# A feed-forward stage on one core: gate-up products in seven block products instead of eight, down projections in a second half

## What is computed

```python
h = h + mixed @ w_out
hn = rms_norm(h, ffn_norm_g)
h = h + (silu(hn @ w_ffn_gate) * (hn @ w_ffn_up)) @ w_ffn_down     # 1024 -> 2816 -> 1024
y = rms_norm(h, final_norm_g)
```

## Time and profile before

| what | us |
|---|---|
| median of 3 runs (3351.07 to 3356.76) | 3355.32 |
| the profiled execution's own time | 3351.76 |
| its span in the trace | 3350.0 |

### The profile page before, as it was taken

How to read it: one execution, slowest core, us unless ns; L and a number is a source line. 1 busy time by engine, 2 the same in 40 slices (tenths; PEclk the granted TensorE clock), 3 DMA queues, 4 the chain that set the end, 5 groups by cost and what they waited for, 6 DMA issues and landing times.

```text
span 3350.0 us, 48536 instructions
## 1 busy us (share of the span) xinstructions
PE 3205.6 (96%) x19989; PEld 2651.2 (79%) x19989; DVE 1698.0 (51%) x3486; ACT 1203.4 (36%) x2403; POOL 548.2 (16%) x797
## 2 busy tenths in 40 slices
PE   8999999999999989899889999899999999999998
PEld 6888888888887767787667788778888788888886
DVE  3544445354454736536653898676653343334234
ACT  4542443344344433323452132566622311111113
POOL 0230131122022513203342132000020000000000
PEclk9999999999999989999989999999999999999999
DMA  3113112211311021131112132100043311111111
GB/s 104 39 39 120 38 46 73 72 33 53 111 65 39 20 91 45 70 138 33 51 66 77 58 94 82 45 1 1 1 176 114 120 51 51 44 45 51 51 51 51
DMA packets 59479, 210.12 MB, mean 63 GB/s; under 512 B 7015, under 2 KB 11721, under 8 KB 54522
## 3 DMA queue, kind: packets, MB, share of 16 engines
q1 hardware_dynamic: 59258, 207.02, 17.7%
HBM read 161.91 MB, written 45.09 MB: 62 GB/s over the span
## 4 chain that ended last, share of the span: by engine, by line
PE 88%; DVE 4%; ACT 4%; POOL 2%; issue 1%; DMA 1%; SPq 0%; POOLq 0%; DVEq 0%; ACTq 0%
PE pp L632 11%; PE pp L633 11%; PE pp L635 11%; PE pp L1238 9%; PE pp L1239 9%; PE pp L1240 9%; PE pp L805 2%; PE pp L807 2%; PE pp L806 2%; PE pp L1211 2%; PE pp L1195 2%; PE pp L763 1%; PE pp L733 1%; PE pp L747 1%; PE pp L1203 1%
## 5 line engine op out<-in xcount | busy, mean ns | idle before, releaser
L632 PE MATMUL pp<-gx_hi,pw_hi 128*128 128x512 f32 x1504 | 616.0, 410 | 22.0 <-DVE pw_lo L1955 22.0
L635 PE MATMUL pp<-gx_hi,pw_lo 128*128 128x512 f32 x1504 | 593.5, 395 | 0.0
L633 PE MATMUL pp<-gx_lo,pw_hi 128*128 128x512 f32 x1504 | 593.1, 394 | 0.0
L632 PEld LDWEIGHTS pp<-gx_hi,pw_hi 128*128 128x128 f32 x1504 | 286.8, 191 | 87.4 <-DVE pw_lo L1955 22.7
L635 PEld LDWEIGHTS pp<-gx_hi,pw_lo 128*128 128x128 f32 x1504 | 286.2, 190 | 62.7
L633 PEld LDWEIGHTS pp<-gx_lo,pw_hi 128*128 128x128 f32 x1504 | 287.2, 191 | 55.1
L1238 PE MATMUL pp<-mix_hi,wt_hi 128*128 128x512 f32 x704 | 274.1, 389 | 2.8 <-DVE arena L2616 1.6
L1239 PE MATMUL pp<-mix_lo,wt_hi 128*128 128x512 f32 x704 | 273.9, 389 | 0.0
L1240 PE MATMUL pp<-mix_hi,wt_lo 128*128 128x512 f32 x672 | 261.4, 389 | 0.0
L1928 ACT ACTIVATE xT<-pp 128x1024 f32<-128x1024 f32 x22 | 22.6, 1029 | 535.3 <-PE pp L1240 535.3
L2648 DVE TENSOR_TENSOR xT<-xT,pp 128x1024 f32<-128x1024 f32 x22 | 26.9, 1221 | 368.7 <-ACT xT L1928 368.7
(11 more groups left out here) (510 smaller groups left out, 6819.9 us busy)
## 6 DMA issues: line engine op xcount, KB each, us to landing
arena<-in_tiles_dram SPq DMA_DIRECT2D x73, 512.0 KB, 3.5
arena<-in_units_dram SPq DMA_DIRECT2D x33, 1024.0 KB, 4.8
y_scratch<-y SPq DMA_DIRECT2D x48, 512.0 KB, 2.9
y<-y_scratch SPq DMA_DIRECT2D x40, 512.0 KB, 4.4
xT<-in_tiles_dram SPq DMA_DIRECT2D x27, 512.0 KB, 4.2
xT<-in_w_outs_dram SPq DMA_DIRECT2D x12, 1024.0 KB, 7.1
arena<-gates_scratch SPq DMA_DIRECT2D x16, 512.0 KB, 3.7
xT<-in_wall_dram SPq DMA_DIRECT2D x3, 2048.0 KB, 9.7
```

The lines of the kernel that those rows point to most:

```text
L632: mm(b[:, hs], wh[:, c], X[0][:, k, hs], k == 0, False)
L633: m = mm(b[:, hs], wh[:, c], X[1][:, k, hs], False, both and k == 7)
L635: m = mm(b[:, hs], wl[:, c], X[0][:, k, hs], False, k == 7)
```

## The change

Each gate-up tile is a product of 2x2 blocks: the weights are A11 and A12 (gate, first and second 512 inputs) and A21 and A22 (up), the activations B11, B12 (first 512 inputs, first and second 512 tokens) and B21, B22. Winograd's form of Strassen's scheme makes it of seven block products, each 4 x 3 = 12 matmuls into one bank, with sums before and after:

- weights, VectorE, per tile, 128x512 each: ssum = A21+A22, a21 := A11-A21, a11 := ssum-A11, a12 := A12-a11
- activations, once, on quarters of 256 tokens (128x4x256): T1 = B12-B11 (VectorE), T3 = B22-B12, T2 = B22-T1, T4 = B21-T2 (GpSimd), then all split into high and low parts
- results, per tile, 128x512 each: ScalarE copies products 1 and 5 out of PSUM; VectorE forms U2, U3, both gates and the near up; GpSimd adds U2 to the far gate and U3 to the copy of product 5
- each tile's result goes raw through DRAM (`a_scratch`); the down projections run after all tiles, in 22 steps of 48 matmuls (11 pairs for tokens 0 to 511, then 11 for 512 to 1023), and sum over the 11 pairs in eight PSUM banks

The diff, cut to its core ("..." marks what is left out):

```diff
 def unit_plan():
-    plan = [("gu", 0)]
...
+    return [("gu", j) for j in range(FF_TILES)] + [("dn", i) for i in range(FF_TILES // 2)]
...
+        products = {1: (W_first, 0, "B11", 0), 2: (W_first, 512, "B21", 0), 5: (W_sum, 0, "T1", 1), 3: (W_rest, 512, "B22", 1),
+                    6: (W_rest, 0, "T2", 2), 4: (W_rest, 1536, "T4", 2), 7: (W_rest, 1024, "T3", 3)}
...
         def pe_program(e):
...
+            def product(j, p):
+                left, c, right, spot = products[p]
+                i = ([2, 3, 0, 1] if j % 2 == 0 else [4, 5, 6, 7])[spot]
+                if p in (1, 5, 6, 7):
+                    place_(Ring([i]), ("gb", j, spot), {1: ("c11", j), 5: ("c13", j), 6: ("c21", j), 7: ("u3", j)}[p])
+                pe.wait_ge({1: ("wlA", j), 2: ("wlA", j), 5: ("wl1", j), 6: ("wlS", j, 0), 3: ("wlS", j, 0), 7: ("wlS", j, 1),
+                            4: ("wlS", j, 1)}[p])
+                pe.wait_ge({2: ("p1c", j), 3: ("p5c", j), 4: ("u2", j)}.get(p))
+                pe.wait_ge([("tl", right, 0), ("tl", right, 1)] if right[0] == "T" or right == "B22" else None)
+                for k in range(4):
...
+                    m = passes(bank[i], left[j % 2], [a[:, k, :] for a in BP[right]], slice(c + k * 128, c + k * 128 + 128),
+                               slice(0, 512), k == 0, k == 3)
+                m.then_inc(*did("gp", j, p))
+            product(0, 1)
+            product(1, 1)
+            turn(7)
+            product(0, 2)
+            product(1, 2)
+            product(0, 5)
+            product(1, 5)
+            for j in range(2):
+                for p in (7, 3, 6, 4):
+                    product(j, p)
+            for j in range(2, FF_TILES):
+                for p in (1, 5, 6, 7, 2, 3, 4):
+                    product(j, p)
+            def down(s):
+                th, i = divmod(s, ff_steps // 2)
+                pe.wait_ge(("dal", s), ("dwl", s))
...
         def act_program(e):
...
+            def down_high(s):
+                i = s % (ff_steps // 2)
+                ac.wait_ge(("al", s), ("gp", 20, 4) if s == 0 else [("a", 21, 0), ("a", 21, 1), ("c22", 21)] if s == 1 else step_end(s - 2))
+                act(a_parts[s % 2][0], a_place[s % 2], ACT.Copy).then_inc(*did("dah", s))
+                ac.wait_ge(("unit", FF_TILES + i), ("gp", 20, 4) if s == 0 else ("gp", 21, 4) if s < 3 else step_end(s - 3))
+                act(w_parts[s % 3][0], w_place[i], ACT.Copy).then_inc(*did("dwh", s))
...
+                if n == 7:
+                    first_high(1)
...
+            token_high("T1", 0)
+            copy_1(0)
+            sum_high(0)
+            token_high("B22", 0)
+            copy_1(1)
+            token_high("T3", 0)
+            rest_high(0, 1)
+            rest_high(0, 0)
+            token_high("T1", 1)
...
+            for s in range(ff_steps):
+                if s + 1 < ff_steps:
+                    down_high(s + 1)
+                if s % (ff_steps // 2) == ff_steps // 2 - 1:
+                    for n in range(4):
+                        final(s // (ff_steps // 2) * 4 + n)
...
         def dve_program(e):
...
+            def second(j):
+                dv.wait_ge(("p1c", j), ("gp", j, 6), ("a", j - 1, 0) if j else [("hf", 7), ("hst", 7)])
+                tt(U2, P1c[j % 2], at("gb", j, 2), ALU.add).then_inc(*did("u2", j))
+            def near_(j):
+                dv.wait_ge(("gp", j, 4), ("u3", j), ("c12", j))
+                tt(U2, U3, at("gb", j, 2), ALU.add).then_inc(*did("c21", j))
...
+            token_low("T1", 0)
+            sum_low(0)
+            first_sum(1)
+            token_low("B22", 0)
+            turn(7)
+            token_first(1)
+            token_low("T1", 1)
+            sum_low(1)
+            token_low("T3", 0)
+            rest_low(0, 1)
+            rest_low(0, 0)
+            token_low("B22", 1)
+            token_low("T3", 1)
+            token_low("T2", 0)
+            token_low("T2", 1)
+            other_sums(1)
+            token_low("T4", 0)
+            token_low("T4", 1)
+            second(0)
+            third(0)
+            rest_low(1, 1)
+            rest_low(1, 0)
+            far_gate(0)
+            near_gate(0)
+            near_(0)
+            far(0)
...
+            for j in range(2, FF_TILES):
+                more = j + 1 < FF_TILES
+                if more:
+                    first_low(j + 1)
+                    first_sum(j + 1)
+                    other_sums(j + 1)
+                    sum_low(j + 1)
+                second(j)
+                if more:
+                    rest_low(j + 1, 0)
+                third(j)
+                if more:
+                    rest_low(j + 1, 1)
+                else:
+                    down_low(0)
+                near_gate(j)
+                far_gate(j)
+                near_(j)
+                far(j)
...
         def pool_program(e):
...
-            for n in range(8):
+            for n in range(7):
                 rms(n)
+            token_third(0)
+            rms(7)
+            token_second(0)
+            token_fourth(0)
+            token_third(1)
+            token_second(1)
+            token_fourth(1)
+            for j in range(FF_TILES):
+                far_gate(j)
+                far_up(j)
...
         def sp_program(e):
...
+            used(0)
+            unit(2)
+            for j in range(FF_TILES):
+                if j + 1 < FF_TILES:
+                    used(j + 1)
+                    unit(j + 3)
+                if j == FF_TILES - 1:
+                    sp.wait_ge(("gp", j, 4))
+                    unit(24)
+                    a_in(1)
+                store(j)
+                if j == FF_TILES - 2:
+                    a_in(0)
```

More of the change, by code:

```diff
@@ L460, in program, with four @@
-        AA = [[over(f"a{i}_{c}", 1024, F32R, base, o + j * 1024) for j, c in enumerate(("hi", "lo"))]
-              for i, (base, o) in enumerate((("w1", 0), ("w1", 2048), ("xT", 0)))]
-        sg = [SL[0][:, 2048 + i * 1024:3072 + i * 1024] for i in range(2)]
-        order = unit_plan()
-        last_aa = [over(f"al_{c}", 1024, F32R, "arena", 13696 + (len(order) - 2) % 2 * 2048 + j * 1024) for j, c in enumerate(("hi", "lo"))]
-        def halves_of(j):
-            return last_aa if j == FF_TILES - 1 else AA[j % 3]
+        def four(name, base, at):
+            return by_four(over(name, 2048, F32R, base, at))
@@ new lines, in by_four @@
+        def by_four(a):
+            return a.rearrange("p (k t) -> p k t", k=4)
+        BP = {"B11": [a[:, 0:4, 0:512] for a in (MH, ML)], "B21": [a[:, 4:8, 0:512] for a in (MH, ML)],
+              "T1": [a[:, 0:4, 512:1024] for a in (MH, ML)], "B22": [a[:, 4:8, 512:1024] for a in (MH, ML)]}
+        for name, base in (("T3", "w2"), ("T2", "w3"), ("T4", "w1")):
+            BP[name] = [four(name + "_hi", base, 0), four(name + "_lo", base, 2048)]
+        near, far = (slice(0, 512), slice(512, 1024))
@@ new lines, in program @@
+        BR_raw = {"T1": (0, near), "T2": (0, near), "T3": (0, far), "T4": (1, near), "B22": (1, far)}
+        W_first = [[over(f"wa{i}_{c}", 1024, F32R, base, o + j * 1024) for j, c in enumerate(("hi", "lo"))]
+                   for i, (base, o) in enumerate((("arena", 8192), ("xT", 4096)))]
+        W_sum = [[over(f"w1{i}_{c}", 512, F32R, "xT", 6144 + i * 1024 + j * 512) for j, c in enumerate(("hi", "lo"))] for i in range(2)]
+        W_rest = [[over(f"ws{i}_{c}", 2048, F32R, base, j * 2048) for j, c in enumerate(("hi", "lo"))]
+                  for i, base in enumerate(("w0", "xT"))]
@@ L589, in program, with step_end @@
         attn_done = [("ot", 63), ("ao", 31), ("oT", 63), ("aT", 31), ("oa", 31)]
[L590 to L597, removed]
+        mixed = ("m2", 7, 1)
+        def step_end(s):
+            return ("dn", 0, 3, 1) if s == ff_steps // 2 - 1 else ("ds", s)
+        xs_done = [("xsl", k) for k in range(8)]
         def pe_program(e):
@@ L1284, in pe_program @@
             mix_order(mix1, turn, mix2, skip)
[L1288 to L1302, removed]
@@ L1314, in down @@
[L1314 to L1320, removed]
+                            c = x_ * 512 + n * 128
+                            m = passes(bank[2 * n + hf], a_parts[s % 2], w_parts[s % 3], slice(c, c + 128), slice(o, o + 512),
+                                       i == 0 and x_ == 0, i == ff_steps // 2 - 1 and x_ == 1)
@@ L1854, in rms, with split_x @@
             def rms(n):
+                if n == 7:
+                    first_high(1)
                 rms_rows(n, yrow[n % 2], hnf[n % 2], ff_tiny[n % 2], "hf", ("y3", n, 0), ("y3", n, 1), ("hfT", n - 2, 1) if n >= 2 else ("mix", 7))
[L1857 to L1864, removed]
+            def split_x(k):
+                ac.wait_ge([("xf", n, k // 4) for n in range(4)], ("m2", 3, 1))
+                act(xs[0][0][:, k, :], xk[k][:, 0:512], ACT.Copy).then_inc(*did("xsh", k))
@@ new lines, in token_high @@
+            def token_high(name, q):
+                x_, c = BR_raw[name]
```

(37 more changed lines are left out.)

268 lines of the change are left out of this document (201 added, 67 removed).

## The result

| | kernel before | changed kernel |
|---|---|---|
| median, us | 3355.89 (4 runs, 3351.07 to 3356.76) | 3309.78 (4 runs, 3303.22 to 3316.16) |
| profiled execution: own time, span | 3351.76, 3350.0 | 3303.22, 3301.3 |

The ratio is 0.9865, 95% interval 0.9839 to 0.9892: 1.35% faster, 46 us. The forecast was 3304 for the median and 3302.0 for the profiled execution, which took 3303.2.

What follows compares the result with a forecast made beforehand. TensorE's matmul count, plus stalls at seams, was taken as the bound. Terms -54.4 - 2.6 + 1.0 + 2.8 - 4.4 + 7.8 = -49.8 us gave 3302.0 profiled, median 3304; 8-in-10 range 3290 to 3322.

Steps and rivals of the forecast that it cites:

- The tiles: Tiles 2 to 21: 84 matmuls in place of 96, 19.04 us per tile, 2.72 less, -54.4 us in all.
- The cover: In each tile, VectorE and GpSimd work of 14.4 us at worst hides behind TensorE's 19.04; cost 0.
- The rival that they would: Product starts in new banks cost time through waits or clock falls: +18 to +40 us, 3322 to 3344; chance 0.08.
- The rival of VectorE as the bound: In the tile loop VectorE's waits line up in a chain; at 22.5 us per tile +69, 3373; chance 0.05.
- The start: From turn(6) to tile 2: TensorE idles 6.4 us before product 5, 5.2 before product 7; in all +7.8 us.
- hidden in the second wait: Tile 0: the clock fall after product 5's wait costs nothing, absorbed before product 7; only the second fall costs, +1.8 us.
- The two waits before product 4: In tiles 0 and 1, product 4 waits 0.9 and 1.7 us for VectorE's U2.
- The rival that the start is hidden: GpSimd holds VectorE less in the hand-over: start -3.5 in place of +7.8 us, time 3293; chance 0.13.
- The end: After TensorE's last matmul: the span ends 9.6 us later in place of 14.0, -4.4 us.
- The down part: Down projections, same 1056 matmuls: -2.6 us for stalls removed, +1.0 and +2.8 for two uncovered seams.
- the row-3 hiccups: Old down units: each loses 0.24 us at its third row behind VectorE's split; removing 11 gives -2.6 us.
- steps 1 and 12: Down part: late activations cost +1.0 us (0 to 4.2) at 1, final rows ahead of splits +2.8 (0 to 6) at 12.

Runs made afterwards that it cites:

- e6: Changed kernel with VectorE's two splits of the weights' rest each repeated twice more per tile, from tile 2 on; time 3307.1 us.
- e7: Changed kernel with VectorE's two splits of the weights' rest each repeated five times more per tile, from tile 2 on; time 3437.0 us.
- e2: Changed kernel with GpSimd's sums T3 (second quarter), T2 and T4 cut to one column, order and waits unchanged; one time, 3291.86 us.
- e3: Changed kernel with the activations of down step 1 loaded before the wait for the last product and weight unit 24; one time, 3297.16 us.
- e5_start: Changed kernel with five GpSimd activation sums moved to VectorE and the hand-over re-ordered; median 3294.33 us, ratio 0.9829 to the kernel before.
- e0_after: The changed kernel run again with no edit, as yardstick; median 3305.19 us, ratio 0.986 to the kernel before.

## Why the prediction was right

**The tiles.** 20 tiles in 381.0 us, 19.05 each, against 19.04. The cover was judged right, and with a margin: 4.9 us more of VectorE's work per tile did no harm (e6), and by e7 VectorE needs 13.3 of the 19.05, where the prediction's bound from adding it all up was 14.4. One slip in its walk through the tile changed nothing: in the order 1, 5, 6, 7, 2, 3, 4, products 2 and 3 start at 10.9 and 13.6 and not at 13.6 and 16.3, and their copies, made by 6, still have 5 us. The hand-overs cost nothing. The rival that they would is out for this kernel: clock 1.00 in all three full stretches of 100 us, with 154 products. The Trainium skill (TensorE: Matmul & The Clock Gate, section "A second HAM failure mode: psum-queue depth-cycling") reports a kernel whose clock swung between its levels as its groups of matmuls cycled through PSUM banks; the stretches above, at 12 matmuls a bank, and the earlier trace rows, at 6 in the down units, do not show that. The rival of VectorE as the bound needed a period of VectorE over 21.4 us, where its own part was 13.3; e7 shows what it looks like.

**The start.** The chain of VectorE and GpSimd was forecast to have T1's second half ready 19.3 us after turn(6), it took 19.4 (2626.48 - 2607.07); T3's 30.0, it took 30.1 (2637.13). The wait before product 7 was 2.7 and not 5.2, for TensorE itself came later: the two products ahead ran their first matmuls at the lower clock, which the prediction had put in words ("hidden in the second wait") but not in the wait's length. The two waits before product 4 were 0.78 and 1.30, against 0.9 and 1.7. The sum, +7.8 against +7.7, doesn't depend on it. The rival that the start is hidden needed GpSimd not to hold VectorE; it did, and e2 shows what the start would be without: waits of 1.2 and 0.6.

**The end.** -4.4, as forecast; all eleven traces of the changed kernel and its variants end 9.6 us behind TensorE's last matmul, to 0.1.

**The down part** is the one term that was missed: +5.4 in place of +1.2. Both stalls were at their places, and the 2.6 us of the row-3 hiccups did go. But steps 1 and 12 cost 3.8 and 4.2 in place of 1.0 and 2.8. Of the 4.2 us by which the term was missed, 1.0 is the load: step 1's activations landed about 7.5 us behind the last product, where 6.5 was taken. The 0.5 MB were queued behind 1 MB and beside two stores; which of them made it longer was not tested, e3 shows only that the landing sets the wait. The other 3.2 are the clock, for the price of a wait was put at its length alone. Behind each of the two, TensorE ran seven matmuls or so at 0.427:

```profile
3178.26 0.39 PE L1252 MATMUL pp<-wd_hi,ap_lo 128*128 128x512 f32 x1
3181.18 0.79 PE L1250 MATMUL pp<-wd_hi,ap_hi 128*128 128x512 f32 x1 [2.53 <-DVE wd_lo L2773]
3181.77 0.63 PE L1251 MATMUL pp<-wd_lo,ap_hi 128*128 128x512 f32 x1
3182.20 0.63 PE L1252 MATMUL pp<-wd_hi,ap_lo 128*128 128x512 f32 x1
...
3184.28 0.39 PE L1251 MATMUL pp<-wd_lo,ap_hi 128*128 128x512 f32 x1
3184.51 0.40 PE L1252 MATMUL pp<-wd_hi,ap_lo 128*128 128x512 f32 x1
```

That is the timeline of TensorE of the changed kernel at step 12: 0.43 from start to start (1.2 GHz), and 0.23 (2.4 GHz) from 3184.28 on. The prediction charged this price only for the two waits of 5 and 6 us in the start.

**The number.** The profiled execution missed by 1.2 us, of which -3.2 lie ahead of turn(6), where nothing changed, and +4.2 in the down part: two misses that cancel, so that it came within 1.2 is luck. On the median the forecast was 5.8 low, inside what the runs spread.

## What to carry to other kernels

When one engine is full and the others are half idle, a scheme that trades its instructions for theirs is worth the distance from start to start times the number removed, here 2.72 us per tile to 0.5%. Its costs were here not in the loop but at the seams, where the new preparation runs before there is work to hide it; walk each seam's queue in order, engine by engine, and count a GpSimd operation with SBUF inputs as VectorE's time too where VectorE has an operation with two SBUF inputs beside it. Measure the cover by adding work to the covered engine until the time moves.

## What the runs showed that was not expected

**The same wait is not always followed by the lower clock.** The wait before step 12 was 2.53 to 2.57 us in nine traces; in four of them (the changed kernel, e3_step1, e5_start, e7_dve_plus5) six to eight matmuls ran at 0.43 behind it, in five none. The same program, in e0_after:

```profile
3182.11 0.39 PE L1252 MATMUL pp<-wd_hi,ap_lo 128*128 128x512 f32 x1
3185.04 0.50 PE L1250 MATMUL pp<-wd_hi,ap_hi 128*128 128x512 f32 x1 [2.54 <-DVE wd_lo L2773]
3185.38 0.39 PE L1251 MATMUL pp<-wd_lo,ap_hi 128*128 128x512 f32 x1
3185.61 0.40 PE L1252 MATMUL pp<-wd_hi,ap_lo 128*128 128x512 f32 x1
```

Before step 1, where the wait was 1.81 to 2.05 us in eight traces, the clock fell in five. A fall costs 1.4 to 1.8 us (3.8 us lost with, 2.1 without, at step 1). After the 6.5 us wait it fell in each of the eight traces that have that wait. What decides it after the short waits is open.

**Ahead of the stage** the same instructions ended between 2604.9 and 2612.4 us (turn(6), eleven traces of the changed kernel and its variants, which are the same up to there), and the kernel before ranged from 3339.9 to 3356.9 in twenty-one runs. It has many waits of 1 us and more up to there, the longest 14.4. The granted clock between 100 and 200 us was 1.00 in e3_step1 (turn(6) at 2604.9) and 0.98 in e6_dve_plus2 (2612.1), but also 0.98 in the changed kernel (2607.1) and 1.00 in the kernel before (2610.3). So falls of the clock taken or missed may be part of this spread, but that stretch does not set it alone, and no run tested it.
